# Splitting GpSimd's value differences of two cache pages into two instructions of one page each

## The reference

```python
kp = cache_k[i, page_table].reshape(db, past_len, MOBA_HEADS, HEAD_DIM)
...
gate = jnp.einsum('bhtd,bhnd->bhtn', qh.astype(jnp.float32), k_mean)
...
_, sel = lax.top_k(gate, n_sel)
...
p = jax.nn.softmax(logits.reshape(bsz, h, qc, r * MOBA_BLOCK), axis=-1).reshape(logits.shape)
return jnp.einsum('bhqrs,bhqrsd->bhqd', p, vg.astype(jnp.float32)).astype(q.dtype)
```

## Time and profile before

| | |
|---|---|
| median of 3 runs | 1305.23 us (1303.71 to 1305.43) |
| profiled execution | 1302.96 us, its span 1301.2 us |
| TensorE products busy | 1143.8 us (88%) |
| TensorE weight loads busy | 1005.1 us (77%) |
| VectorE busy | 722.9 us (56%) |
| ScalarE busy | 563.0 us (43%) |
| GpSimd busy | 294.1 us (23%), of which line 594: 145.0 us |
| page transfers | 128 of keys and 128 of values, 256 KB each |

### The profile page before, as it was taken

How to read it: one execution, slowest core, us unless ns; L and a number is a source line. 1 busy time by engine, 2 the same in 40 slices (tenths; PEclk the granted TensorE clock), 3 DMA queues, 4 the chain that set the end, 5 groups by cost and what they waited for, 6 DMA issues and landing times.

```text
span 1301.2 us, 20535 instructions
## 1 busy us (share of the span) xinstructions
PE 1143.8 (88%) x7143; PEld 1005.1 (77%) x7143; DVE 722.9 (56%) x1216; ACT 563.0 (43%) x886; POOL 294.1 (23%) x262
## 2 busy tenths in 40 slices
PE   5999689778788788767989999997999799999995
PEld 4999689455455454443889999996999699999994
DVE  4743624566656766642466666345556566666333
ACT  3447301344454555433364444335334554443434
POOL 8201015101454554453220000022101310000011
PEclk9999959888989999985989999998999899999997
DMA  7334100335657666735425345343444244544421
GB/s 229 114 103 157 35 1 1 119 133 186 210 196 242 226 207 215 246 110 162 135 85 174 129 139 181 116 134 118 129 153 149 95 130 147 175 129 135 151 78 40
DMA packets 119124, 182.62 MB, mean 140 GB/s; under 512 B 6128, under 2 KB 59471, under 8 KB 118990
## 3 DMA queue, kind: packets, MB, share of 16 engines
q1 hardware_dynamic: 116274, 173.30, 40.6%
q0 software_dynamic: 2784, 8.47, 2.4%
HBM read 176.12 MB, written 5.63 MB: 140 GB/s over the span
## 4 chain that ended last, share of the span: by engine, by line
PE 46%; ACT 3%; DVE 2%; POOL 1%; issue 0%; DVEq 0%; POOLq 0%
PE bank L1618 46%; POOL xl L617 1%; ACT xres L953 1%; DVE xres L1068 1%; ACT hi L674 1%; ACT xh L674 1%; PE bank L2015 0%; ACT L944 0%; PE bank L2083 0%; DVE xres L1480 0%; DVE hraw L1068 0%; PE bank L2005 0%; DVE lo L1061 0%; DVE lnt L1068 0%; ACT lnt L946 0%
## 5 line engine op out<-in xcount | busy, mean ns | idle before, releaser
L1618 PE MATMUL bank<-xh,hi 128*128 128x320 f32 x1184 | 373.7, 316 | 40.0 <-POOL xl L617 26.4
L1618 PE MATMUL bank<-xl,hi 128*128 128x320 f32 x1184 | 371.3, 314 | 0.0
L1618 PE MATMUL bank<-xh,lo 128*128 128x320 f32 x1184 | 370.9, 313 | 0.0
L1061 DVE TENSOR_TENSOR lo<-raw,hi 128x2048 fp32r<-128x2048 f32 x102 | 241.3, 2366 | 188.6 <-ACT hi L674 188.6
L1618 PEld LDWEIGHTS bank<-xh,hi 128*128 128x128 f32 x1184 | 227.5, 192 | 43.1 <-issue 31.2
L674 ACT ACTIVATE hi<-raw 128x2048 fp32r (+1 forms) x102 | 194.8, 1909 | 107.6 <-PE bank L1618 107.6
L1618 PEld LDWEIGHTS bank<-xl,hi 128*128 128x128 f32 x1184 | 227.5, 192 | 0.1
L1618 PEld LDWEIGHTS bank<-xh,lo 128*128 128x128 f32 x1184 | 227.2, 192 | 0.0
L594 POOL TENSOR_TENSOR lo<-vring,hi 128x1024 fp32r<-128x1024 f32 x60 | 145.0, 2418 | 176.1 <-ACT hi L674 176.0
L1068 DVE TENSOR_TENSOR kTl<-bank,kTh 128x512 fp32r<-128x512 f32 x128 | 88.1, 689 | 103.6 <-ACT kTh L674 101.6
L1618 PE MATMUL bank<-hh,hi 128*128 128x320 f32 x416 | 129.3, 311 | 1.3 <-DVE hraw L1068 1.3
(11 more groups left out here) (376 smaller groups left out, 1500.1 us busy)
## 6 DMA issues: line engine op xcount, KB each, us to landing
raw<-w_up SPq DMA_DIRECT2D x44, 1024.0 KB
kring<-cache_k SPq DMA_DIRECT2D x128, 256.0 KB, 3.7
vring<-cache_v SPq DMA_DIRECT2D x128, 256.0 KB, 3.4
raw<-w_down SPq DMA_DIRECT2D x8, 2048.0 KB
raw<-w_in_mix SPq DMA_DIRECT2D x7, 2048.0 KB
raw<-w_in_sc SPq DMA_DIRECT2D x8, 1024.0 KB
raw<-w_down SPq DMA_DIRECT2D x4, 1536.0 KB
raw<-w_out_mix SPq DMA_DIRECT2D x2, 2048.0 KB
```

The lines of the kernel that those rows point to most:

```text
L1061: dve.tensor_tensor(lo[:, p], weight(n)[:, :, 256 * p:256 * p + 256], hi[:, p], ALU.subtract)\
L1618: return pe.matmul(out, lhsT, rhs, start=start, stop=stop, **kw)
```

## The change

GpSimd's difference of a unit, one instruction of 128 x 1024, becomes two of 128 x 512, one for each page, in order. The semaphore is raised by the second alone. The four units that VectorE makes are left as they are.

```diff
                 w = n % 2
                 pool.wait_ge(s["v_hi"], n + 1)
-                pool.tensor_tensor(vl[:, w], vring[:, n // 2 % 2, 2 * w:2 * w + 2, :], vh[:, w], ALU.subtract)\
-                    .then_inc(s["v_lo"], 1)
+                for j in range(2):
+                    ins = pool.tensor_tensor(vl[:, w, j], vring[:, n // 2 % 2, 2 * w + j, :], vh[:, w, j], ALU.subtract)
+                ins.then_inc(s["v_lo"], 1)
```

## The result

| | before | after |
|---|---|---|
| median | 1302.37 us (1299.86 to 1306.05, 9 runs) | 1307.60 us (1305.67 to 1310.51, 9 runs) |
| profiled execution, span | 1301.2 us | 1305.4 us |
| line of the value difference | 60 instructions, 145.0 us busy | 120 instructions, 152.4 us busy |

The ratio is **1.0037 (interval 1.0021 to 1.0052)**: slower by 4.8 us, 2.7 to 6.8. The median of before fell from the 1305.23 us of three runs to 1302.37 of nine, so the predicted 1308.2 lies near the measured time partly because its base stood too high; the predicted difference was +3.0 us.

The account below looks back on a forecast made before the run. The bound was taken as a loop of GpSimd's difference, the in-order transfer queue and TensorE's key-page waits; 1.44 + 0.24 + 0.12 + 1.2 = +3.0 us on the median 1305.23 gave 1308.2 us, range 1304.6 to 1310.5.

Parts of the forecast that it names:

- The half's price: GpSimd's value difference: 512 columns take 0.19 + 1.10 = 1.29 us; with 0.07 overlap a pair costs +0.12 us.
- The arcs: Rounds with key pages: 12 chains from GpSimd's end through the queue to TensorE, each 0.12 later, +1.44 us.
- the last round: Two units back to back, 565.01 to 569.72: two longer pairs delay VectorE's copies and weight difference, +0.24 us.
- the 583.05 unit: After the last round: TensorE waits once for the first unit of the pair at 583.05, +0.12 us.
- the last unit: Last two units: VectorE takes the port between GpSimd's halves, TensorE resumes at 610.6 instead of 609.36, +1.2 us.
- the rival of shorter halves: GpSimd's difference: two halves together shorter than the whole, 14 x -0.56 = -7.8 us, 1297.4 us; chance 0.05.
- its 1.1 us for the port: Last two units: the part of +1.2 us from VectorE taking the port between halves; without it +0.12.
- a rival that it would not: Last units: GpSimd keeps the port through both halves, last term 0.12, sum +1.9 us, 1307.1 us; chance 0.20.
- Small instructions of VectorE costed at nothing: Each round's copies and comparisons: +0.15 to +0.25 us each, covered by TensorE's 0.75 us wait for key pages.
- The race: At 572.67 us GpSimd's unit beats VectorE's weight difference to the port: +1.4 for +0.24, sum +4.2 us; chance 0.26.
- Relief of VectorE: Rounds: VectorE regains half of the 1.45 + 1.83 us lost to whole instructions, sum -1.5 us, 1303.7 us; chance 0.07.
- What would show it: Signs in the profile after, among them the stretch between key-page waits of 337.86 and 549.40 longer by 1.3 us.

Follow-up runs that it names:

- memsets: Kernel before, whole differences, semaphore raised only after small one-column memsets: ratio 1.0024 with four, 1.0075 (1.0052 to 1.0097) with 14.
- quarters: Kernel before with every GpSimd difference unit in four instructions of 256 columns: ratio 1.0072 (1.0047 to 1.0097).

## Why the prediction was right or wrong

- *The half's price*, 0.19 + 1.10: right, 1.287 us. The overlap was too large by half: the 0.07 of the earlier trace rows is 0.04 between halves. By the Trainium skill (GPSIMD Engine Reference, section 3.1) the fixed part was estimated at 0.28 us, from the page's 2048 columns and the trace's 1024; the 0.18 of the rows above decides against it.
- *The arcs*: right, the mechanism and, as far as one profile of each kernel shows it, the count. Lateness from memsets costs the same time as from quarters, shortening the queue's part of the same chain gave 29 us, and the time without a product grew in the rounds by about 11 times the lateness. With the pair at its measured +0.14 the prediction's own places (12 arcs, two pairs in the last round, the 583.05 unit, the last unit: 16, where the rival of shorter halves says 14) and its 1.1 us for the port give 3.3 us, inside the measured 2.7 to 6.8.
- **What the sum left out is the granted clock.** It is shown as a part of the cost where the lateness is 0.4 us. The measured costs are 22 to 26 us per us of lateness, where the 16 places would give 16; all four rows taken as independent give 20 to 29, an estimate. At 0.40 us the places give 6.4 us, and the clock's 0.0027 less goes with 2.4 more: 8.8 against 9.8 measured (6.8 to 12.6). At the quarters' 0.43 it is 6.9 + 1.1 = 8.0 against 9.4 (6.1 to 12.6). For the halves alone the share of the clock isn't resolved: the nine runs had 0.9333, and the runs of before beside the experiments 0.9339. That the whole excess lies at the end is excluded: with the last 12 units whole the cost was 3.3 us (0.7 to 5.9).
- *One reading of the end was short*: after the last round TensorE was said to wait for GpSimd at the 583.05 pair and at the last unit only. In the profile of before its products waited for GpSimd four times between 550 and 612 us, until 567.44, 585.45, 602.87 and 609.36:

```profile
PE bank L1618 <- POOL lo L594: 7.9, 4, 2.8
```

  Behind the 602.87 wait the next rounding stood 3.79 us for its pages (605.82), so not each of them need reach the end. By the profiles the end grew by some 3.3 us, where the sum has 1.6; with a scatter of 4 us the size stays open.
- *The last round*, +0.24 from two pairs: the pairs grew by 0.26 as said. *The 583.05 unit*, +0.12: not resolved by any run.
- *The last units*, +1.2: the port does pass to VectorE between halves (the prediction had as a rival that it would not), on one of the last two pairs in each of four profiles, which makes that pair about 0.94 us longer than 2.53. That it comes to 1.2 us of the whole time isn't shown, as the last 12 units alone cost 1.4 us (-1.7 to +4.4).
- *Small instructions of VectorE costed at nothing*: right, 2.10 and 2.23 us against 2.08 and 2.25, even without the 0.15 to 0.25 that were put in for the slip.
- *The race*, the rival with +4.2, which lies nearest the measured difference: **right in the profile, wrong as a cause.** Its premise, that before VectorE wins, came from one execution. VectorE usually loses with whole instructions too, the change with unit 54 left whole is as slow, and with the race taken away from both, the halves still cost 3.3 us (0.8 to 5.7).
- *Relief of VectorE* and *shorter halves*: fell, by the same 2.1 and 2.2 us and by 1.287 against the 1.23 that was named. The quarters do relieve VectorE by some 1.1 us a round, and their time is no better than that of the 14 memsets, which don't.
- *What would show it*: the stretch between the key waits was to grow by 1.3 us and in the profile of after it shrank, 211.54 to 210.86. That test was not fit: unchanged rounds gave 206.9 to 212.7 us in five profiles. The time without a product in the same stretch would have been: 34.0 to 36.9 us in those five, 37.4 to 38.5 with halves.
- *Luck*: the predicted time is 0.6 us from the measured one because the base stood 2.9 us too high and the difference was forecast 2.2 us too low (3.0, where the medians lie 5.2 apart).

## What to carry to other kernels

An instruction off the busy engine can still be priced by its end: look for who waits on its semaphore, and what an in-order queue holds back behind that wait. Then the fix lies less in the instruction than in the queue, here: reading addresses ahead, and releasing a buffer in the pieces in which it comes free, was worth 29 us where the split had cost 5. A wait of TensorE can cost more than its length, since the products behind it may run at the lower clock; compare the time without a product, and the products' own time, one by one. An event seen in one profile, two starts 0.01 us apart above all, is a draw and no property of the kernel; profile the kernel before twice before a term rests on it.

## What the runs showed that was not expected

Small instructions on GpSimd are nearly free behind a large one: 14 memsets of one column took 0.47 us together, 0.03 apiece, though one alone is shown with 0.10. Four key pages let TensorE go on 5.8 to 6.9 us after their issue in the first profile of before. Without any edit in the rounds the stretch between the first and the last key wait moved by 5.8 us from profile to profile, more than the change did there; about half of that is TensorE's own busy time (172.9 to 176.1 us at a granted clock of 0.95 to 0.94), and half is time without a product.
